# Layer norm behind a depthwise convolution: token sums as one-column matmuls among the taps, mean and root spread from four columns

## The reference, cut to what matters

```python
def conformer_conv(u, rows, w_pw1, b_pw1, w_dw, b_dw, ln_g, ln_b, w_pw2, b_pw2):
    a = u @ w_pw1 + b_pw1
    a = a[..., :CONV_DIM] * jax.nn.sigmoid(a[..., CONV_DIM:])
    ...
    a = dwconv(...)                                   # 31 taps per feature
    a = jax.nn.silu(layer_norm(a + b_dw, ln_g, ln_b)) # over the 1024 features of a token
    return a @ w_pw2 + b_pw2
```

## Time and profile before

| | us |
|---|---|
| median of three runs | 3057.93 (3056.44 to 3058.35) |
| the profiled execution, its time | 3059.75 |
| its span in the trace | 3057.9 |
| PE busy in the span | 2969.5 |
| DVE busy | 2088.8 |
| ACT busy | 1189.9 |

### The profile page before, as it was taken

One profiled execution on the slowest core, in us unless ns is written; L12 is line 12 of the kernel. 1 busy time (PEld: TensorE's weight loads), 2 busy tenths in 40 slices (PEclk: granted clock), 3 DMA queues, 4 the chain that ended last, 5 costly groups with the idle time before them and its releaser, 6 DMA issues.

```text
span 3057.9 us, 41784 instructions
## 1 busy us (share of the span) xinstructions
PE 2969.5 (97%) x15114; PEld 2464.7 (81%) x15114; DVE 2088.8 (68%) x3193; ACT 1189.9 (39%) x1806; POOL 179.0 (6%) x148
## 2 busy tenths in 40 slices
PE   7999999999999999998999999999999999999998
PEld 5888578888877799876888888788878878986897
DVE  6973588877785766797798886566654632646755
ACT  3223424332154654554342323452244422423553
POOL 1300000000011000000030210000000000001120
PEclk9999999999999999999999999999999999999999
DMA  7562054666523156310256451672256622442554
GB/s 275 196 238 97 21 199 172 214 206 235 198 95 104 63 189 222 120 56 28 83 192 213 164 195 61 213 255 104 104 197 222 222 83 97 156 177 90 193 186 145
DMA packets 125377, 479.84 MB, mean 157 GB/s; under 512 B 13768, under 2 KB 13768, under 8 KB 122912
## 3 DMA queue, kind: packets, MB, share of 16 engines
q1 hardware_dynamic: 119232, 443.60, 42.0%
q0 software_dynamic: 5984, 34.04, 3.0%
HBM read 459.76 MB, written 17.83 MB: 156 GB/s over the span
## 4 chain that ended last, share of the span: by engine, by line
PE 82%; DVE 11%; ACT 3%; issue 3%; DMA 1%; SPq 1%; DVEq 0%; ACTq 0%
PE bank L775 24%; PE bank L777 24%; PE bank L776 24%; PE bank L1669 2%; PE bank L1054 1%; ACT w_hi L1737 1%; DVE tmp L3392 1%; DVE w_lo L2422 1%; PE bank L1637 1%; DVE x_res L2524 1%; ACT tmp L1737 1%; DVE x_res L2530 1%; DMA ada_first<-in_ada 0%; PE bank L1435 0%; PE bank L1436 0%
## 5 line engine op out<-in xcount | busy, mean ns | idle before, releaser
L2422 DVE TENSOR_TENSOR w_lo<-w_raw,w_hi 128x1024 fp32r<-128x1024 f32 x617 | 752.3, 1227 | 578.2 <-ACT w_hi L1737 563.5
L1737 ACT ACTIVATE w_hi<-w_raw 128x1024 fp32r<-128x1024 f32 x620 | 648.7, 1054 | 704.0 <-PE bank L777 678.3
L775 PE MATMUL bank<-h_hi,w_hi 128*128 128x512 f32 (+1 forms) x2008 | 693.9, 346 | 26.3 <-DVE h_lo L3136 7.3
L776 PE MATMUL bank<-h_lo,w_hi 128*128 128x512 f32 (+1 forms) x2008 | 687.2, 342 | 0.0
L777 PE MATMUL bank<-h_hi,w_lo 128*128 128x512 f32 (+1 forms) x2008 | 686.8, 342 | 0.0
L775 PEld LDWEIGHTS bank<-h_hi,w_hi 128*128 128x128 f32 x2008 | 382.1, 190 | 78.4 <-issue 23.8
L776 PEld LDWEIGHTS bank<-h_lo,w_hi 128*128 128x128 f32 x2008 | 382.0, 190 | 45.1 <-issue 1.2
L777 PEld LDWEIGHTS bank<-h_hi,w_lo 128*128 128x128 f32 x2008 | 381.9, 190 | 43.6
L775 PE MATMUL bank<-w_hi,xm_hi 128*128 128x512 f32 x512 | 200.9, 392 | 0.0
L777 PE MATMUL bank<-w_hi,xm_lo 128*128 128x512 f32 x512 | 199.4, 389 | 0.0
L776 PE MATMUL bank<-w_lo,xm_hi 128*128 128x512 f32 x512 | 199.3, 389 | 0.0
(11 more groups left out here) (450 smaller groups left out, 5071.4 us busy)
## 6 DMA issues: line engine op xcount, KB each, us to landing
w_raw<-in_weights SPq DMA_DIRECT2D x620, 512.0 KB, 3.5
ada_ring_f<-in_ada SPq DMA_DIRECT2D x56, 512.0 KB, 3.3
ada_ring_g<-in_ada SPq DMA_DIRECT2D x44, 512.0 KB, 3.3
ada_ring_b<-in_ada SPq DMA_DIRECT2D x38, 512.0 KB, 4.2
ada_ring_a<-in_ada SPq DMA_DIRECT2D x32, 512.0 KB, 3.4
ada_first<-in_ada SPq DMA_DIRECT2D x16, 512.0 KB, 15.3
v_spill<-ml_v POOLq DMA_DIRECT2D x4, 1024.0 KB, 4.9
o_spill<-ml_o_grp POOLq DMA_DIRECT2D x4, 1024.0 KB, 4.6
```

Source lines behind the costliest of these rows:

```text
L775: mm(out, lhs[0], rhs[0], start=start, stop=False)
L776: mm(out, lhs[0], rhs[1], start=False, stop=False)
L1737: return nc.scalar.activation(out, in_, func, **kw)
L2422: V.tensor_tensor(WLO[:, slot, :], RAW[:, slot, :], WHI[:, slot, :].bitcast(F32), SUB)\
```

## The change

The sums over features are turned round. In `conv_sum` the data is the stationary operand, 128 tokens at a time, and a single column of ones is moved through: the result is one column in bank 6, with tokens on the partitions. Eight such calls per chunk (four blocks of tokens, plain and squared) replace one product of 512 columns with ones for the plain sum and one for the squares. The calls of chunks 0 to 3 stand among the taps of chunks 4 to 6, those of chunks 4 to 6 among the taps of chunk 7, those of chunk 7 behind them. ACT squares each chunk (`conv_square`) between its weight tiles. Since the squares are now taken before the mean is known, a shift, chunk 0's mean over its features, is subtracted: `conv_shift` on PE gives it, from chunk 2 on DVE subtracts it in the tap with j = 1, and chunks 0 and 1 are corrected during chunk 3.

Behind the last chunk, mean, variance, root and reciprocal are four columns wide (`C_MEAN` and so on in `FUSE`). Diagonal matrices of them, times ones, give back rows in banks 7 (mean) and 5 (root) (`conv_spread`). DVE centres and normalises from there; bank 5 is copied to `tmp(2)` after the first chunk, and PE's first group of pw2 waits for the two banks (`spread_left`). The low part of chunk c - 1 now stands behind the normalisation of chunk c, one chunk sooner than before. `PE_TAPS` of chunk 7 goes from 16 to 14. `turn_over(4)` ahead of chunk 7's taps goes to 0; `turn_over(3, 1)` and `turn_over(6, 1)` are put around `conv_spread`. `lo_ahead` for the first three weight tiles of pw2's second part stands among the residual steps instead of behind them.

```diff
 CONV_W, CONV_ROWS = 31, LAT // GRID_W
-PE_TAPS = [12] * 7 + [16]
+PE_TAPS = [12] * 7 + [14]
+SHIFT_FROM = 2
 PE_TAPS_MAX = max(PE_TAPS)
...
                 last.then_inc(S("tile_done"), 1)
-            def conv_taps(p):
+            def conv_taps(p, sums=()):
                 if p >= 2:
...
                 if p == 0 or p == DC - 1:
-                    turn_over(4 if p else 5, conv_bank(p))
+                    turn_over(0 if p else 5, conv_bank(p))
                 pe.wait_ge(S("conv_diag_done"), p + 1)
...
                                     j == 0, j == PE_TAPS[p] - 1)
-                last.then_inc(S("conv_pe_done"), 1)
-            def conv_feature_sum(c):
-                pe.wait_ge(S("conv_z_done"), c + 1)
-                last = mm(PS[6][:, :], ONES[:, :], CZ[:, c, :], start=c == 0, stop=c == DC - 1)
-                if c == DC - 1:
-                    last.then_inc(S("ln_sum_done"), 1)
+                    if j == PE_TAPS[p] - 1:
+                        last.then_inc(S("conv_pe_done"), 1)
+                    per = min(2, len(sums))
+                    for n in range(per * j, min(per * j + per, 8 * len(sums))):
+                        conv_sum(sums[n // 8], n % 8)
+            def conv_shift():
+                pe.wait_ge(S("conv_z_done"), 1)
+                mm(PS[7][:, :], ONES[:, :], CZ[:, 0, :], start=True, stop=True).then_inc(S("conv_shift"), 1)
+            def conv_sum(c, n):
+                square, b = n // 4, n % 4
+                if n == 0 and c < SHIFT_FROM:
+                    pe.wait_ge(S("conv_shifted"), N("conv_shifted", c + 1))
+                elif n == 0:
+                    pe.wait_ge(S("conv_z_done"), c + 1)
+                elif n == 4:
+                    pe.wait_ge(S("sq_done"), 4 * DC + c + 1)
+                part = (tmp(c % 2) if square else CZ[:, c, :])[:, b * P:(b + 1) * P]
+                last = mm(PS[6][:, n:n + 1], part, ONES[:, 0:1], start=c == 0 and n == 0, stop=c == DC - 1 and n == 7)
+                if n == 7:
+                    last.then_inc(S("sq_used"), 1)
+            def conv_spread():
+                pe.wait_ge(S("mean_diag"), N("mean_diag", 1))
+                for b in range(4):
+                    last = mm(PS[7][:, b * P:(b + 1) * P], ONES[:, :], tmp(1)[:, b * P:(b + 1) * P], start=True, stop=True)
+                last.then_inc(S("mean_rows"), 1)
+                for b in range(4):
+                    pe.wait_ge(S("root_diag"), N("root_diag", b + 1))
+                    last = mm(PS[5][:, b * P:(b + 1) * P], ONES[:, :], tmp(0)[:, b * P:(b + 1) * P], start=True, stop=True)
+                last.then_inc(S("root_rows"), 1)
+            def spread_left(o):
+                if o == 5:
+                    pe.wait_ge(S("root_copied"), N("root_copied", 1))
+                if o == 7:
+                    pe.wait_ge(S("z_centered"), DC)
             for s in range(LOOKAHEAD):
...
                 if t % 2 == 0:
-                    conv_taps(t // 2 - 1)
-                    if t >= 6:
-                        conv_feature_sum(t // 2 - 3)
-            conv_feature_sum(DC - 3)
-            conv_taps(DC - 1)
-            for c in range(DC - 2, DC):
-                conv_feature_sum(c)
-            square_sums(4, TOK, 7)
-            pe.wait_ge(S("std_done"), 5)
-            half_cols("pw2", HHI, HLO, "cz_lo_done", 0, None, 2, 2, lambda i: ln_steps(i, 2, 32))
+                    conv_taps(t // 2 - 1, {10: (0, 1), 12: (2,), 14: (3,)}.get(t, ()))
+                    if t == 4:
+                        conv_shift()
+            conv_taps(DC - 1, (4, 5, 6))
+            for n in range(8):
+                conv_sum(DC - 1, n)
+            turn_over(3, 1)
+            conv_spread()
+            turn_over(6, 1)
+            half_cols("pw2", HHI, HLO, "cz_lo_done", 0, spread_left, 2, 2, lambda i: ln_steps(i, 2, 32))
             def tok_block(ph, hi, lo, half, s, t, stop):
...
                 last.then_inc(S("conv_diag_done"), 1)
+            def conv_square(c):
+                if c < SHIFT_FROM:
+                    act.wait_ge(S("conv_shifted"), N("conv_shifted", c + 1))
+                else:
+                    act.wait_ge(S("conv_z_done"), c + 1)
+                if c >= 2:
+                    act.wait_ge(S("sq_used"), 4 * DC + c - 1)
+                f(tmp(c % 2), CZ[:, c, :], ACT.Square).then_inc(S("sq_done"), 1)
             act.wait_ge(S("conv_w_lo_done"), N("conv_w_lo_done", 1))
...
                         .then_inc(S("pw1_gate_free"), 1)
+                    for c in {8: (0, 1), 10: (2,), 12: (3,), 14: (4, 5)}.get(t, ()):
+                        conv_square(c)
                 else:
...
                         conv_diag(p + 1)
-            squares(4, TOK, CZ, "z_centered", 0, 7)
+            conv_square(DC - 2)
+            f(CELL[:, 1:2], ONES[:, 0:1], ACT.Sqrt)
+            conv_square(DC - 1)
+            act.wait_ge(S("conv_var"), N("conv_var", 1))
+            f(C_STD, C_VAR, ACT.Sqrt, bias=vec("eps", 1)).then_inc(S("std_done"), 1)
+            act.wait_ge(S("rstd4_done"), N("rstd4_done", 1))
+            for b in range(4):
+                f(tmp(0)[:, b * P:(b + 1) * P], IDENT[:, :], ACT.Copy, scale=C_RSTD[:, b:b + 1])\
+                    .then_inc(S("root_diag"), 1)
+            f(CELL[:, 1:2], ONES[:, 0:1], ACT.Silu)
             for c in range(DC):
...
                 dve.wait_ge(S("x_upd"), 8 * (ln + 4) + (0 if ln == 1 else 8))
-                dve.wait_ge(S("ln_sum_done"), ln + 1)
+                dve.wait_ge(S("ln_sum_done"), ln)
                 own(V.tensor_scalar(tmp(2)[:, C_COLS], PS[3][:, L_COLS], 1.0 / D, None, MUL))
...
                 conv_input(p)
+                if p == SHIFT_FROM:
+                    dve.wait_ge(S("conv_shift"), N("conv_shift", 1))
+                    own(V.tensor_scalar(tmp(2), PS[7][:, :], 1.0 / P, None, MUL))
+                shift = tmp(2).rearrange("p (r w) -> p r w", w=GRID_W)
                 acc0, acc1 = CACC[:, 2 * (p % 2), :], CACC[:, 2 * (p % 2) + 1, :]
...
                         ins = V.tensor_scalar(acc, x_j, w_j, vec("b_dw", p), MUL, ADD)
+                    elif j == 1 and p >= SHIFT_FROM:
+                        ins = V.scalar_tensor_tensor(acc, x_j, w_j, shift, MUL, SUB)
                     elif j == 1:
...
                         conv_lo(p)
+                    if j == 2 and p == SHIFT_FROM + 1:
+                        for c in range(SHIFT_FROM):
+                            V.tensor_tensor(CZ[:, c, :], CZ[:, c, :], tmp(2), SUB).then_inc(S("conv_shifted"), 1)
                 dve.wait_ge(S("dve_own"), own.at)
...
                 V.tensor_tensor(CZ[:, p, :], acc0, PS[3 * (p % 2) + 2][:, :], ADD).then_inc(S("conv_z_done"), 1)
-            dve.wait_ge(S("conv_z_done"), 8)
-            layer_norm(0, 4, TOK, CZ, 6)
-            for c in range(DC + 2):
+            dve.wait_ge(S("sq_used"), 5 * DC)
+            own(V.tensor_scalar(C_MEAN, PS[6][:, 0:4], 1.0 / D, None, MUL))
+            own(V.tensor_tensor(C_SQ, C_MEAN, C_MEAN, MUL))
+            V.scalar_tensor_tensor(C_VAR, PS[6][:, 4:8], 1.0 / D, C_SQ, MUL, SUB).then_inc(S("conv_var"), 1)
+            for b in range(4):
+                if b == 2:
+                    dve.wait_ge(S("std_done"), 5)
+                    V.reciprocal(C_RSTD, C_STD).then_inc(S("rstd4_done"), 1)
+                last = V.tensor_scalar(tmp(1)[:, b * P:(b + 1) * P], IDENT[:, :], C_MEAN[:, b:b + 1], None, MUL)
+            last.then_inc(S("mean_diag"), 1)
+            dve.wait_ge(S("mean_rows"), N("mean_rows", 1))
+            def conv_center(c):
+                V.tensor_tensor(CZ[:, c, :], CZ[:, c, :], PS[7][:, :], SUB).then_inc(S("z_centered"), 1)
+            conv_center(0)
+            conv_center(1)
+            dve.wait_ge(S("root_rows"), N("root_rows", 1))
+            for c in range(DC + 1):
                 if c < DC:
-                    V.tensor_tensor(CZ[:, c, :], CZ[:, c, :], tmp(2), MUL).then_inc(S("cz_norm"), 1)
-                if c >= 2:
-                    dve.wait_ge(S("cz_hi_done"), c - 1)
-                    V.tensor_tensor(HLO[:, c - 2, :], tmp(c % 2), HHI[:, c - 2, :].bitcast(F32), SUB)\
+                    dve.wait_ge(S("z_centered"), c + 1)
+                    V.tensor_tensor(CZ[:, c, :], CZ[:, c, :], tmp(2) if c else PS[5][:, :], MUL)\
+                        .then_inc(S("cz_norm"), 1)
+                    if c == 0:
+                        V.tensor_copy(tmp(2), PS[5][:, :]).then_inc(S("root_copied"), 1)
+                        dve.wait_ge(S("root_copied"), N("root_copied", 1))
+                if c + 2 < DC:
+                    conv_center(c + 2)
+                if c >= 1:
+                    dve.wait_ge(S("cz_hi_done"), c)
+                    V.tensor_tensor(HLO[:, c - 1, :], tmp((c - 1) % 2), HHI[:, c - 1, :].bitcast(F32), SUB)\
                         .then_inc(S("cz_lo_done"), 1)
...
             for c in range(DC):
+                if c % 3 == 0:
+                    lo_ahead("pw2", c // 3, c // 3)
```

(13 more changed lines are left out.)

## The result

| | us |
|---|---|
| before, median of 11 | 3056.86 (3055.33 to 3058.76) |
| changed, median of 11 | 3064.52 (3059.24 to 3066.53) |
| changed / before | 1.0021, 95% interval 1.0013 to 1.0029 |
| changed, the profiled execution | 3059.24, span 3057.3 |
| changed again (run `after_again`), median of 10 | 3064.39; its profiled execution 3065.50, span 3063.6 |

The medians differ by 7.7 us: the change costs 0.2% where 0.1% (3.5 us) gained was forecast. Both are shown, because what differs between them is the answer.

A forecast was written before the change was run, and what follows sets the result against it. PE, busy 97% of the span, was taken as the bound. 6.3 us gained without the clock, less 2.8 for clock falls, left 3.5 off the median 3057.93: 3054.4 us, chance 0.50, range 3048.5 to 3061.5.

The forecast's parts named there:

- The price of a call: One-column sums among the taps on PE: 0.22 us per call, two weight loads 0.11 apart.
- Tile 15: The pw1 tile on PE ahead of the last taps: ends 3.6 us later.
- C: End of the last `conv_z` addition, behind chunk 7's taps: forecast to come 7.5 us later.
- pw2's first matmul: Start of pw2 on PE, behind the tail: at C + 9.9 instead of C + 20.1.
- The reordered low parts: At pw2's fourth group: the 2.41 us hole and its slow matmuls, 1.6 us, would be gone.
- The sum without the clock: Start of pw2's fourth group, counted at full clock: 42.5 - 28.7 - 7.5 = 6.3 us gained.
- The wait at bank 7: PE before output 7 of pw2's first group: stands 2.3 us until the eighth chunk is centred.
- The rival in which DVE paces pw2 at 0.76: DVE's new loop takes 0.76 us per operation, not 0.65; bank 7 wait 1.9 us longer, 3056.3 us; chance 0.16.
- hidden or dear loads: One-column calls cost 0.11 us each (3048.2 us, chance 0.12) or 0.38 each (3064.6 us, chance 0.10).
- part 3: Clock falls: 1.4 us ahead of the last taps, 0.6 around C, 0.8 before pw2 and at bank 7; 2.8 together.
- the eight matmuls above: First eight matmuls of pw2's fourth group in the kernel before: 0.43 us apart where 0.23 is usual, 1.6 us lost.
- The slower rival: Calls between the last taps cost both loads in full, 0.38 us each: 10.2 us more, 3064.6 us; chance 0.10.

The follow-up runs named there:

- quick execution: First profiled execution of the unaltered changed kernel, the quickest of its eleven: 3059.24 us.
- usual one: Profiled execution of the changed kernel run again unaltered: 3065.50 us.
- fill7: Changed kernel with turn_over(7) in place of turn_over(0) ahead of the last taps: 3051.22 us, 0.9980 of before.
- fill7_tail: fill7 with turn_over(2, 1) added ahead of chunk 7's one-column sums: 3050.35 us, 0.9978 of before.
- sums_behind: Changed kernel with the 24 calls of chunks 4 to 6 moved from among the last taps to behind them, idle time kept: 3055.82 us, 0.9995 of before.
- fill4: Changed kernel with turn_over(4) put back ahead of the last taps: 3052.33 us, 0.9989 of before.
- no_fill_before: Kernel before with turn_over(0) in place of turn_over(4) ahead of the last taps: 3058.01 us, 1.0003 of before.
- sums_first: Changed kernel with the 16 calls of chunks 4 and 5 moved into the idle time ahead of the last taps: 3049.83 us, 0.9974 of before.
- sums_first_12: sums_first with two of the last chunk's taps moved from PE to DVE (`PE_TAPS` 12): 3049.67 us, 0.9976 of before.

## Why the prediction was wrong

Times are counted from DVE's input step of chunk 7, since the quick execution of the changed kernel was 1.3 us ahead before any changed instruction (the `w_lo` step that precedes the first convolution chunk starts at 1273.63, in before at 1274.94), and the usual one 1.9 us (1273.05).

**Right.** The price of a call: pairs 1.15 apart less a tap's 0.72 leave 0.22 for each of two calls, as worked out from the earlier trace rows. The instructions stand 0.11 apart. The Trainium skill, "TensorE: Matmul & The Clock Gate", section "Back-to-back issue gap", would have made it 0.16 by my estimate; its 81 ns are for a matmul of 128 columns, and the trace disagrees for this call of one column. Tile 15: the input step came 1415.80 - 1413.51 = 2.3 us later in an execution that was 1.3 ahead, 3.6 in all, as said (usual: 1.7 + 1.9, the same). C at full clock: 19.9 behind the input step was forecast, fill7 has 1435.12 - 1415.36 = 19.8. pw2's first matmul at C + 9.9: 1443.94 - 1434.03 = 9.9 in fill7_tail. The reordered low parts: 4.0 forecast, 3.9 measured. The sum without the clock, 6.3 us gained: fill7_tail is 6.8 us under the before beside it, 3057.14, or 0.22%. That this fits so well is in part luck, since its profile lacks the low stretch near 1695, 1.7 us that the sum did not count.

**Slightly off.** The wait at bank 7 was 1.5 us and not 2.3, since DVE's loop has a pitch of 0.60 where I took 0.65. The rival in which DVE paces pw2 at 0.76 did not occur, nor did hidden or dear loads.

**Wrong: part 3.** "I count a fall to 1.2 GHz there, 1.4 us (up to the 1.6 of the eight matmuls above)". The place was right, PE idle 3.38 us, and the sign. The size was not: the last taps took 28.5 us in a usual execution and 15.3 at full clock, 13.2 us against 1.4. This is the step that failed, the price of the fall in front of the last taps. I took the length of the low stretch from the earlier trace rows, where wide matmuls alone follow the fall, and carried it to a place where every tap is followed by two one-column calls. sums_behind shows taps alone paying 3.41 us at 1.2 GHz, 1.7 us lost, near my figure. The rest of the tail paid about 3 us in a usual execution, 1460.70 - 1447.83 = 12.9 from C to pw2 instead of 9.9, where I had 0.6 and a part of 0.8. Put together: 13.2 + 3.0 lost against 2.8 forecast is 13.4 too little; 0.8 of bank 7 goes the other way, and so does 1.7 for the low stretch near 1695 that the profile of before had and the usual one has not. That leaves 10.9, where the median missed by 10.1 (3064.5 against 3054.4): near enough for profiles of single executions.

None of the rivals was this one. The slower rival had a like time, 3064.6, by dear loads at 0.38; the runs exclude it, since fill4 pays 0.22. The range ended at 3061.5 because the clock's price was bounded by 2.8 and its absence only, and not by the case that the low clock lasts as long as the mixed stretch.

The same step seen from the kernel before: I asked what idle time costs where wide matmuls follow it, not what the new work behind it would make of a fall. no_fill_before shows that the same edit costs the old kernel nothing, with 2.33 us idle.

**Open.** Why the fall among taps with calls ends after 13.65 us, in the middle of them, in one profile, and only behind `turn_over(3)` in the other; what in such a mixture brings the clock back (with two calls to a tap it came back in one profile of two, with one call to a tap in both, sums_first and sums_first_12, after 6.83 us); what starts the short falls behind C, which some profiles have and others of the same code do not; and whether the two taps of sums_first_12 are worth anything in the median.

## What to carry to other kernels

A clock fall costs what it lasts, and how long it lasted here depended on the work behind it: price it over the whole stretch of work up to the next run of wide matmuls, not by the falls seen elsewhere. In this kernel narrow matmuls between wide ones were cheap only when little idle time stood ahead of them; fill it, best with such narrow work and a few wide matmuls among it, since narrow work alone brought a fall of its own (sums_first). When a wait is removed, look for the idle time that it leaves in front of the next stretch.
